# A two-block transformer kernel: x's chunks 33 lines apart, and the arena four lines behind the weights

## What is computed

```python
for l in range(DEPTH):                       # DEPTH = 2, first_block
    x = x + 0.5 * swiglu(rmsnorm(x, ffn1_norm[l]), w_ffn1_in[l], w_ffn1_out[l])
    u = rmsnorm(x, mix_norm[l])
    c_q, c_kv, k_r, hq, hf, hi, hgate, mq, gate_logits = split_sizes(u @ w_in[l], IN_SPLITS)
    ...
    merged = gates[:, :, 0] * y_mla + gates[:, :, 1] * y_hg + gates[:, :, 2] * y_mem
    x = x + merged @ w_out[l]
    x = x + 0.5 * swiglu(rmsnorm(x, ffn2_norm[l]), w_ffn2_in[l], w_ffn2_out[l])
```

## Time and profile before

| | |
|---|---|
| median of 3 runs | 2441.47 us (2440.64 to 2442.57) |
| profiled execution | 2440.76 us |
| its span, first to last instruction | 2439.0 us |
| PE busy | 2417.3 us, 20238 matmuls |
| DVE, ACT, POOL busy | 1787.9, 1200.7, 114.7 us |
| DMA, mean over the span | 167 GB/s |

### The profile page before, as it was taken

The page is one execution under the profiler, slowest core; times in us unless marked ns, Lnnn a source line. Parts: engine busy times, 40 slices in busy tenths (PEclk is TensorE's granted clock), DMA queues, the critical chain, the costliest instruction groups (busy, mean ns, idle before and its releaser), DMA issues.

```text
span 2439.0 us, 46973 instructions
## 1 busy us (share of the span) xinstructions
PE 2417.3 (99%) x20238; PEld 2238.2 (92%) x20238; DVE 1787.9 (73%) x1606; ACT 1200.7 (49%) x1207; POOL 114.7 (5%) x74
## 2 busy tenths in 40 slices
PE   9999999999999999999999999999999999999998
PEld 7999999999989999999999999998998999998997
DVE  7877767777786768777767777867767777867765
ACT  5445655544454456565445444735445444735443
POOL 0000251000000003500000000000000000000000
PEclk9999999999999999999999999999999999999999
DMA  8555444555555554445555555513655655513652
GB/s 282 192 189 182 128 154 139 173 184 186 186 184 182 189 175 141 139 139 167 196 189 173 183 190 170 173 38 122 200 184 169 203 189 167 173 38 122 198 184 101
DMA packets 322767, 406.68 MB, mean 167 GB/s; under 512 B 6480, under 2 KB 291152, under 8 KB 322384
## 3 DMA queue, kind: packets, MB, share of 16 engines
q1 hardware_dynamic: 321488, 400.58, 51.1%
q10 hardware_dynamic: 1152, 4.22, 0.5%
HBM read 403.72 MB, written 1.05 MB: 166 GB/s over the span
## 4 chain that ended last, share of the span: by engine, by line
PE 93%; DVE 4%; ACT 2%; issue 1%; DMA 0%; SPq 0%; DVEq 0%; ACTq 0%
PE ps L344 47%; PE ps L339 45%; DVE w_lo L303 1%; ACT w_hi L298 1%; ACT x_hl L366 1%; DVE sq L401 0%; DVE x_hl L391 0%; DMA raw<-in_w_ffn_in 0%; PE ps L1501 0%; PE ps L2217 0%; ACT sq L370 0%; DVE x L2205 0%; DVE x L642 0%; ACT k_t L1146 0%; DVE m_lo L1268 0%
## 5 line engine op out<-in xcount | busy, mean ns | idle before, releaser
L303 DVE TENSOR_TENSOR w_lo<-raw,w_hi 128x2048 fp32r<-128x2048 f32 x383 | 881.1, 2301 | 263.7 <-ACT w_hi L298 255.9
L344 PE MATMUL ps<-x_hl,w_hi 128*128 128x512 f32 x2816 | 986.2, 395 | 3.0 <-DVE ta L567 1.5
L298 ACT CAST w_hi<-raw 128x2048 fp32r<-128x2048 f32 x383 | 729.2, 1905 | 390.0 <-PE ps L344 195.6
L344 PE MATMUL ps<-x_hl,w_lo 128*128 128x256 f32 x2816 | 782.7, 278 | 0.0
L344 PEld LDWEIGHTS ps<-x_hl,w_hi 128*128 128x128 f32 x2816 | 528.7, 188 | 125.3 <-issue 3.8
L344 PEld LDWEIGHTS ps<-x_hl,w_lo 128*128 128x128 f32 x2816 | 529.5, 188 | 0.4
L339 PE MATMUL ps<-x_hl,w_hi 128*128 128x256 f32 (+1 forms) x2176 | 397.8, 285 | 0.6 <-DVE x_hl L391 0.6
L339 PE MATMUL ps<-h_hi,w_hi 128*128 128x256 f32 x1408 | 395.5, 281 | 0.0
L339 PE MATMUL ps<-h_hi,w_lo 128*128 128x256 f32 x1408 | 393.9, 280 | 0.0
L339 PE MATMUL ps<-h_lo,w_hi 128*128 128x256 f32 x1408 | 393.7, 280 | 0.0
L339 PEld LDWEIGHTS ps<-x_hl,w_hi 128*128 128x128 f32 (+1 forms) x2176 | 339.3, 191 | 4.1 <-issue 2.9
(11 more groups left out here) (462 smaller groups left out, 2733.0 us busy)
## 6 DMA issues: line engine op xcount, KB each, us to landing
raw<-in_w_ffn_in SPq DMA_DIRECT2D x87, 1024.0 KB, 5.1
raw<-in_w_in SPq DMA_DIRECT2D x74, 1024.0 KB, 5.4
raw<-in_w_ffn_out SPq DMA_DIRECT2D x44, 1024.0 KB, 4.8
raw<-in_ffn_w_gate SPq DMA_DIRECT2D x44, 1024.0 KB, 5.3
raw<-in_ffn_w_up SPq DMA_DIRECT2D x44, 1024.0 KB, 5.4
raw<-in_ffn_w_down SPq DMA_DIRECT2D x44, 1024.0 KB, 4.8
raw<-in_w_out SPq DMA_DIRECT2D x16, 1024.0 KB, 4.9
raw<-in_w_mem_kv SPq DMA_DIRECT2D x8, 1024.0 KB, 5.0
```

The costliest lines, as they stand in the source:

```text
L298: nc.scalar.copy(w_hi[:, slot, :], raw[:, slot, :]).then_inc(hi_ready, 1)
L303: nc.vector.tensor_tensor(w_lo[:, slot, :], raw[:, slot, :], w_hi[:, slot, :].bitcast(F32), ALU.subtract).then_inc(lo_ready, 1)
L344: return nc.tensor.matmul(out_ap, l, r, start=first, stop=last, skip_group_check=True)
```

## The change

Two things are placed anew. A chunk of `x_hl` gets 64 bytes more at its end, which nothing reads or writes: chunks are 2112 bytes, 33 lines, apart, so chunk k starts at line 2 + k (modulo 8); its low part still directly follows its high part, and the 512 columns are still contiguous. And `base` is chosen so that the arena starts at line 6 (byte 149,376) in place of line 7. `w_hi`, `w_lo`, `raw` and `x` stay where they are. The instructions of every engine, their order, shapes and waits are the same as before, so no rows of the order are shown.

```diff
@@ -163,6 +163,7 @@
     return at
 
 
+LINE = 16
 COL1, COL2 = columns(VEC1), columns(VEC2)
 VEC_AT = [0, N1, 2 * N1, 2 * N1 + N2]
 N_VEC = DEPTH * (N1 + N2)
@@ -204,8 +205,8 @@
         w_hi = sb("w_hi", [P, SLOTS, UNIT], F32R)
         w_lo = sb("w_lo", [P, SLOTS, UNIT], F32R)
         x = sb("x", [P, DC, T])
-        x_hl = sb("x_hl", [P, DC, 2, T], F32R)
-        x_hi, x_lo = x_hl[:, :, 0, :], x_hl[:, :, 1, :]
+        x_hl = sb("x_hl", [P, DC, 2 * T + LINE], F32R)
+        x_hi, x_lo = x_hl[:, :, 0:T], x_hl[:, :, T:2 * T]
         rms = sb("rms", [P, T])
         rms_col = sb("rms_col", [P, TT])
         var = sb("var", [P, T])
@@ -223,7 +224,7 @@
         lb_small = sb("lb_small", [P, 8, HG_H])
         lb_tmp = sb("lb_tmp", [P, 4, HG_H])
         zero_w = sb("zero_w", [P, P], BF16)
-        base = (nc.sbuf_base + 63) // 512 * 512 + 448
+        base = (nc.sbuf_base - 6 * 64 + 511) // 512 * 512 + 6 * 64
         slots = (nc.sbuf_usable_end - base) // 4096
         arena = sb("arena", [P, slots * 1024 + (base - nc.sbuf_base) // 4])
 
@@ -663,7 +664,7 @@
                         pe.wait_ge(xg_ready, n * 8 + k + 1)
                     for m in range(2):
                         wh, wl = tile3(slot, k * T + m * P, P)
-                        mm(ps[:, bank + m, :], wh, x_hl[:, k, :, :], k == 0, False)
+                        mm(ps[:, bank + m, :], wh, x_hl[:, k, 0:2 * T], k == 0, False)
                         last = mm(ps[:, bank + m, 0:T], wl, x_hi[:, k, :], False, k == DC - 1)
                 last.then_inc(unit_used, 1)
```

## The result

| | median | runs |
|---|---|---|
| before | 2441.57 us | 6 (2440.64 to 2442.96) |
| after | 2451.15 us | 6 (2450.96 to 2452.07) |

The ratio is 1.0039, with a 95% interval of 1.0029 to 1.0049: the change makes the kernel 9.6 us slower. The profiled execution took 2452.07 us, its span is 2450.3 us (before 2439.0), and the granted clock is 0.999.

A forecast was written before the change was run, and what follows sets the result against it. It took PE's matmul spacing as the bound: +12.7 us (arena), -3.9 (x, 256 columns) and +2.1 (pairs) sum to +10.9 us on 2441.5, so 2452.4 us, with 2432 to 2470 us to hold 8 in 10.

The forecast's parts named there:

- the likeliest case: Whole kernel: the sum as worked out, 2452.4 us, with its own range of 2446 to 2460 us; chance 0.48.
- PE's spacing is all of the time: Whole kernel: the time is the summed spacings of about 20,000 matmuls, PE busy 99% of the span.
- The arena, +12.7 us: L339 matmuls with an arena operand (h, m, others): distance 5 to 4 costs each 2.14 ns, 5952 of them.
- Distance 4 costs what distance 0 does: Moving operand starting four lines off the weights (modulo 8) collides as at none; loads 193 and 192 ns at L1563/L1564.
- Distances 2 and 6 no cheaper than the odd ones: Operand two or six lines off the weights: loads not lengthened, but a matmul is now and then; up to +4.6 us.
- Odd ones collide least: Moving operand an odd number of lines off the weights collides least, the collision repeating every four lines.
- x with 256 columns, -3.9 us: L339 matmuls with x: odd chunks, 1824 of 3648, each gain 2.14 ns; the other chunks nothing.
- The pairs, +2.1 us: Hidden layer at L344, 512 then 256 columns: x's changing distance adds 0.5 ns on each of 4224 matmuls.
- The rest at nothing: Matmuls between two arena tiles, DVE and ACT: no cost, at most 0.4 us if PE's cover were gone.
- The rule against it: Skill's rule of separate TensorE read ports: addresses don't matter, so the change costs 0, 2441.5 us.
- The pairs pay too: Rival, L344: x's jump of a line per chunk disturbs the pairs, +21 us at the bound, 2460 us upward; chance 0.18.
- Faster: Rival: x's chunks fall into a quick 113.5 ns spacing, arena matmuls don't collide steadily; 2430 to 2421 us; chance 0.21.

The follow-up runs named there:

- arena_6: Kernel before with only the arena's start moved to line 6 (distance 4 from the weights), x's chunks as before: 2468.37 us, ratio 1.0106.
- arena_2: Kernel before with only the arena's start moved to line 2 (distance 0 from the weights): 2468.42 us, ratio 1.0108.
- arena_1: Kernel before with only the arena's start moved to line 1 (distance 7 from the weights): 2423.29 us, ratio 0.9919.
- arena_5: Kernel before with only the arena's start moved to line 5 (distance 3 from the weights): 2423.34 us, ratio 0.9921.
- arena_4: Kernel before with only the arena's start moved to line 4 (distance 2 from the weights): 2448.48 us, ratio 1.0022.
- x_at_2: Kernel before with only x_hl moved two lines on, all its chunks at distance 2 from the weights: 2446.16 us, ratio 1.0015.
- x_33: Kernel before with only x's chunks set 33 lines apart, the arena staying at line 7: 2440.22 us, ratio 0.9989.
- arena_5_x_3: Kernel before with arena at line 5 and x_hl three lines on, both at distance 3 from the weights: 2442.55 us, ratio 0.9998.
- arena_6_break: arena_6 plus one extra 64 column matmul of zeros ahead of each stretch of pairs that follows h's matmuls: 2461.93 us, ratio 1.0079 against before.
- all_1: Kernel before with weights, x and arena all moved one line on, every distance unchanged: 2442.87 us, ratio 1.0001.

## Why the prediction was right, step by step

The forecast was 2452.4 us and the measured median is 2451.15: slower, within the range and within the likeliest case's own. The term that decides the sign was right in size and, for the arena's own matmuls, in mechanism. Two others were off by about five microseconds each, one each way, and cancelled: that the forecast came within 1.3 us is luck.

- **PE's spacing is all of the time.** Right: PE's busy time and the span moved by 11.0 and 11.3 us, the other engines' share of the chain not at all.
- **The arena, +12.7 us.** Right in place and size. The last 96 matmuls took 11.51 us (forecast 11.5), the loads of h and m went to 192 ns, the means of h's matmuls to 283. Over the trace it is 12.5 us. The count of 5952 lacks the 336 matmuls at L339 whose operand is `c` or `la`, tiles of the arena too; they cost 0.7 of it. arena_6, arena_2 and after have the same 5.75 for 48.
- **Distance 4 costs what distance 0 does.** Shown: arena_6 equals arena_2, and arena_1 equals arena_5. It was inferred from two rows of loads. That was in part luck: with x at 0 the loads tell distances 0 and 4 from the rest and nothing else. The starts in the earlier trace rows spoke less plainly, since six matmuls in 0.70 us are 117 ns each, under the 119.9 of distance 0; half of them have weights 96 wide.
- **Distances 2 and 6 no cheaper than the odd ones.** Borne out for h by arena_4, 118.5 ns against 117.7 at distance 1; for x it is 118.6 at distance 2 (22.78 us for 192), under the 119.9 of 0, where the text put chunks 2 and 6 at nothing. "Odd ones collide least" holds in the means, but an odd distance has two levels 4.2 ns apart, 113.5 and 117.7. This change doesn't depend on it; whoever had looked for the best place from these rows would have missed the 19 us.
- **x with 256 columns, -3.9 us.** The sign was right, the size was not: -9.2. The term gave 2.14 ns to the odd chunks and nothing to the rest. Measured is 2.5 ns on the mean of all 3648. If chunks 2 and 6 gain the 1.3 ns of x_at_2, 1.2 us, the odd ones gain 4.4 ns each, an estimate: part of them runs at the quick level, which the text had only as a bound. The forecast's signs for it were a mean 1 ns lower and loads near 190; they were 3 to 4 ns (282 and 279 for 285 and 283) and a median of 188. x_33 shows the same 22.59 with the arena unmoved. No row separates the chunks.
- **The pairs, +2.1 us.** Sign right, size not: +6.9 (2.5 ns a pair; 2.8 in the stretches shown). I chose 0.5 ns a matmul by the loads, which "have nothing to give back". But the pairs' cost doesn't show in their loads: the mean load on the w_lo side is 189 ns in after and the pair 350.0, against 188 and 347.2. It lies within the 1% that the text allowed, and on 2816 pairs of 347 ns 0.8% is 8 us.
- **The rest at nothing.** Right for DVE and ACT, which moved by 2.2 us of busy time or less, behind PE. All that is neither L339 nor a pair cost 1.1 us.
- **The rule against it.** The Trainium skill, "SBUF — State Buffer", section "Who interferes with whom", gives TensorE's moving operand and its weight loads read ports of their own, independent of each other, and says that PE never waits on anyone. The prediction drew from it that addresses don't matter. The runs don't agree: with the arena's start alone the time goes from 2423.3 to 2468.4 us.
- **The rivals.** "The pairs pay too" was partly true, with 6.9 us and not 21. "Faster" named the quick mode of 113.5 ns, and arena_5 has it for h; but at distance 4 it isn't to be had.

The sum itself had a fault that this change hid. It takes each group's spacing as a function of its own distance. Applied to arena_6 it gives 2454 and misses by 14 us, because h's place changed the pairs' mode; applied to arena_5_x_3 it misses by more than 20. It came out right here since with x's jumping distance the pairs take the same with h at 5 as at 4 (11.21 and 11.20 for 64).

**What stays open.** That a stretch has modes, and that what runs ahead of it picks one, is shown by arena_6_break and all_1. That the thing inherited is a phase between the two streams of reads, and that they collide at all, is argued; no row shows these streams themselves. Nor was it settled why one stretch falls into the quick mode and another doesn't (all_1 starts in the dear one at the distances of before). The executions of before beside arena_6 lie between 2440.47 and 2445.91 us and those of arena_6 between 2467.66 and 2468.49; a feed-forward that changes its mode is worth 352 pairs of 6 ns, about 2 us, so such changes from one execution to the next may be the reason, which no trace shows. Also untried are an extra matmul in arena_5_x_3 and steps smaller than a line.

## What to carry to other kernels

Where TensorE is busy all the time, try where the moving operand starts against the weights, line by line over four lines, one buffer at a time: here that one constant was worth 45 us from worst to best, and the best value lies 19 us under the kernel before. Measure the whole kernel and not the group that was moved, since the effects didn't add here: a place that is good for one stretch can cost the stretch behind it more. Read the spacing from the chain, length over count, since the duration of a weight load didn't tell a good place from a fair one. And where a stretch is dear, look at single starts in it: an average over 65 matmuls hid that all but the first pair had become quick.

## What the hardware showed unexpectedly

- The cost of a place depends on the distance between moving operand and next weights modulo four lines of 64 bytes: 2468.37 against 2468.42 us at distances 4 and 0, 2423.34 against 2423.29 at 3 and 7. With all buffers moved together by a line, the time stays (2442.87 against 2442.50).
- Matmuls of 128 by 128 weights and 256 fp32r columns went at 119.8 to 119.9 ns each with distance 0 or 4, mostly at 118.5 to 118.6 at 2, and at either 113.5 or 117.7 at odd distances (x at 1 and at 3, h at 3; h at 1 only at 117.7), at the full clock. Their weight loads were 192 ns at distances 0 and 4 and 188 or 189 at the others (medians), but a third of h's were at 192 at distance 3 too once x stood at 3 (arena_5_x_3).
- The same pairs (512 and 256 columns) took 347 or 353 ns at the same distances, in one kernel (all_1). One extra matmul of 64 columns ahead of a stretch took its pairs from 353 to 347 ns, to the end of the stretch, and made arena_6 6.4 us faster although it cost about 0.12 us each time.
